# A gate's row loaded behind five adding loads, and new lists of attention pieces, in a two-block transformer kernel

## What is computed

```
log_f = log_sigmoid(f_logit + b_forget)
y_attn = forgetting_attention(q, k, v, log_f) * silu(z_attn)
merged = sigmoid(g_pool) * (y_pool @ w_up_pool) + sigmoid(g_attn) * (y_attn @ w_up_attn)
h = h + merged @ w_out
```

```
x = x + gt1 * (mixed @ w_o)
h = rmsnorm(x, g_norm2) * (1 + sc2) + sh2
x = x + gt2 * (square(relu(h @ w1)) @ w2)
```

## Time and profile before

| | us |
|---|---|
| median of three runs | 997.1 |
| the profiled execution | 995.43 |
| its span, first to last instruction | 993.6 |
| PE busy | 963.2 (97%) |
| weight loads of PE busy | 802.0 (81%) |
| DVE busy | 686.3 (69%) |
| ACT busy | 538.2 (54%) |
| POOL busy | 83.1 (8%) |

### The profile page before, as it was taken

The page is one execution under the profiler, slowest core; times in us unless marked ns, Lnnn a source line. Parts: engine busy times, 40 slices in busy tenths (PEclk is TensorE's granted clock), DMA queues, the critical chain, the costliest instruction groups (busy, mean ns, idle before and its releaser), DMA issues.

```text
span 993.6 us, 13125 instructions
## 1 busy us (share of the span) xinstructions
PE 963.2 (97%) x4712; PEld 802.0 (81%) x4712; DVE 686.3 (69%) x1269; ACT 538.2 (54%) x1053; POOL 83.1 (8%) x173
## 2 busy tenths in 40 slices
PE   8999999999999999999899999999599999999998
PEld 7878999888888888768788878788488888888886
DVE  6487888868788758767678886846244863674773
ACT  6458777753223445589786554356345634643520
POOL 4001001012112011100100000100100000000000
PEclk9999999999999999999999999999799999999999
DMA  8205231248779416452542234224968567583201
GB/s 296 80 23 183 65 106 55 86 188 326 281 287 335 165 71 246 160 158 83 139 142 70 66 98 177 85 85 98 230 208 205 134 208 191 122 237 127 84 32 53
DMA packets 36673, 148.69 MB, mean 150 GB/s; under 512 B 9193, under 2 KB 9193, under 8 KB 24706
## 3 DMA queue, kind: packets, MB, share of 16 engines
q1 hardware_dynamic: 23970, 101.41, 29.3%
q0 software_dynamic: 9568, 42.48, 16.3%
q10 hardware_dynamic: 3072, 3.98, 1.2%
HBM read 138.32 MB, written 5.27 MB: 145 GB/s over the span
## 4 chain that ended last, share of the span: by engine, by line
PE 81%; DVE 9%; ACT 4%; issue 3%; DMA 2%; POOL 0%; SPq 0%; ACTq 0%; DVEq 0%; POOLq 0%
PE psum L2091 24%; PE psum L2093 24%; PE psum L2092 24%; PE psum L2258 2%; PE psum L2237 2%; PE psum L2287 1%; PE psum L2290 1%; DVE wl L1237 1%; DVE two L1776 1%; DMA value_rows<-rows 1%; DVE hl L1277 1%; DVE two L1641 1%; DMA raw<-in_wall 1%; ACT wh L698 1%; DVE xt L1273 0%
## 5 line engine op out<-in xcount | busy, mean ns | idle before, releaser
L2091 PE MATMUL psum<-hh,wh 128*128 128x512 f32 (+1 forms) x720 | 274.0, 381 | 0.7 <-DVE hl L1277 0.6
L2093 PE MATMUL psum<-hh,wl 128*128 128x512 f32 (+1 forms) x720 | 267.3, 371 | 0.0
L2092 PE MATMUL psum<-hl,wh 128*128 128x512 f32 (+1 forms) x720 | 267.3, 371 | 0.0
L1237 DVE TENSOR_TENSOR wl<-raw,wh 128x512 fp32r<-128x512 f32 x328 | 213.9, 684 | 61.0 <-ACT wh L698 60.6
L698 ACT ACTIVATE wh<-raw 128x512 fp32r<-128x512 f32 x328 | 188.9, 620 | 103.9 <-PE psum L2093 68.2
L2091 PEld LDWEIGHTS psum<-hh,wh 128*128 128x128 f32 x720 | 135.3, 188 | 24.4 <-DVE hl L1277 1.4
L2093 PEld LDWEIGHTS psum<-hh,wl 128*128 128x128 f32 x720 | 135.2, 188 | 23.7
L2092 PEld LDWEIGHTS psum<-hl,wh 128*128 128x128 f32 x720 | 135.5, 188 | 21.2 <-issue 1.0
L2091 PE MATMUL psum<-wh,ah 128*128 128x512 f32 x224 | 89.8, 401 | 3.5 <-issue 3.5
L2092 PE MATMUL psum<-wl,ah 128*128 128x512 f32 x224 | 88.3, 394 | 0.0
L2093 PE MATMUL psum<-wh,al 128*128 128x512 f32 x224 | 88.3, 394 | 0.0
(11 more groups left out here) (335 smaller groups left out, 1633.9 us busy)
## 6 DMA issues: line engine op xcount, KB each, us to landing
raw<-in_wall SPq DMA_DIRECT2D x78, 1024.0 KB, 5.3
raw<-in_wall POOLq DMA_DIRECT2D x15, 1024.0 KB, 8.1
wa<-in_wada POOLq DMA_DIRECT2D x24, 512.0 KB, 5.9
gt<-in_wada POOLq DMA_DIRECT2D x20, 512.0 KB, 5.1
xt<-in_xcols SPq DMA_DIRECT2D x8, 264.0 KB, 8.2
cb<-c_rows SPq DMA_DIRECT2D x8, 264.0 KB, 3.6
x<-in_x SPq DMA_DIRECT2D x4, 512.0 KB, 10.2
x_kept<-x SPq DMA_DIRECT2D x4, 512.0 KB, 2.8
```

Of the source, the lines that this page charges most:

```text
L1237: e.tensor_tensor(home(w)[1][:, cs], raw_of(w, c), home(w)[0][:, cs].bitcast(F32), ALU.subtract).then_inc(v["wl"], 1)
L2091: e.matmul(out_, lh, rh, start=start, stop=False, skip_group_check=True)
L2092: e.matmul(out_, lh, rl, start=False, stop=False, skip_group_check=True)
L2093: return e.matmul(out_, ll, rh, start=False, stop=stop, skip_group_check=True)
```

## The change

`gate(1)` leaves its place before the loop over the quarters and goes behind the fifth adding load of the first quarter. The lists `PACE_F` and `PACE_S` are replaced; they hold as many pieces and as many empty beats as before (112 pieces in the first stage, 192 in the second), in the same order, begun in other steps. Of the returned blocks of values the first is subtracted one step later (88), the second nine steps later (97) and the fourth two steps earlier (120).

```diff
-PACE_F = [int(n) for n in ("00000000000000000011140110040102202010113010211101010115131000301121010101301202"
-                           "02000112030230300100300103023301100000110301311112112203021301123113200500330023")]
-PACE_S = [int(n) for n in ("11112111121111211112111121111211112002211200322014011101112010312102222120002304"
-                           "10211203011201010231200160011001211203331201110233120022213230100115031020203441"
-                           "3020305539041021021210001211")]
+PACE_F = [int(n) for n in ("00000000000000001004020200040012202010003300230102200014040001102022000210201301"
+                           "12000211030230300110200104012311000000202202411111110016002301040024300321022024")]
+PACE_S = [int(n) for n in ("11112111121111211112111121111211112013112210021031203200100012302201331210020202"
+                           "01202401003101221111102132111310211312310011034230102004204030201114130121213113"
+                           "1113216547312001203101101111")]
...
-        DV, DV_UPPER, DV_LOWER = (87, 88, 113, 122), (88, 89, 114, 123), (89, 90, 115, 124)
+        DV, DV_UPPER, DV_LOWER = (88, 97, 113, 120), (89, 98, 114, 121), (90, 99, 115, 122)
...
                 e.tensor_tensor(r, r, half[:, 0:1], ALU.pow).then_inc(g["rs3"], 1)
-            gate(1)
...
                 e.wait_ge(v["wl"], 4 * (o + 3) + 4)
                 add(q, 3, a1)
+                if q == 0:
+                    gate(1)
```

## The result

The changed kernel takes 985.75 us, the median of four runs (983.57 to 986.84), against 999.0 (996.34 to 1001.13, four runs) of the kernel before on the same chip: a ratio of 0.9866, 95% interval 0.983 to 0.9902. The forecast was 979.5, range 975 to 985. It is faster, as foreseen, by 13.3 us instead of 17.4, and lies 0.75 us above the range. The forecast started from the three runs named at the top, median 997.1; a fourth took 1001.13 and moved the median to 999.0, so part of the 13.3 us is that start. The profiled execution took 984.85 with a span of 983.1; before it was 995.43 and 993.6, so the span lost 10.5 us where the sum had 17.4.

What follows compares the result with a forecast made beforehand. PE was taken as the bound, so only its idle or slow stretches pay. Gate's row −15.4 and lists −2.0 us took the span from 993.6 to 976.2 and the median from 997.1 to 979.7, stated as 979.5, range 975 to 985.

Steps and rivals of the forecast that it cites:

- The gate's row: MLP's first quarter: with the row behind the adding loads, PE's gaps before P7 and P6 go; −15.4 us, at least 9.
- (c): First quarter: one gap stays because P6's weights are late again, with the slow clock behind; 988.4 us, chance 0.05.
- (d): First quarter: adding loads wait for their plain loads anyway, so nothing moves; 995 to 997 us, chance 0.02.
- (e): Second attention stage: new bursts delay VectorE's weight conversions and PE waits at units of weights; slower, 1001 us, chance 0.03.
- The lists: Attention stages: same work begun in other steps, so only waits differ; −2.0 us in sum, ends −5 and +3.
- The copy `low<-low` holds S8.3 of step 33, which stays where it was: 0: Second attention stage, step 33: the score's wait for its copy of keys stays unchanged; 0 us.
- The returned block comes at about 492 in either case: Second stage: steps 80 to 88 hold ten pieces in both lists, so VectorE is free before T13.3 is turned.
- T13.1: Turn in the second stage, begun in step 94 instead of 91: its 2.0 us of lateness goes; floor of gain 0.
- The wait of S10.3 for `al<-al`: Score of step 49, held 1.0 us by a copy of keys, now begun in step 50; −0.6 us.
- The last head's turns of the first stage: Steps 130 and 131: turns spread one to a step, passing ScalarE's table load; −0.4 us, between −1.3 and +0.7.
- The other waits for `ptl`: Attention stages: last head's turns −0.4 us against +1.0 us for new dense places in steps 40, 85, 169 and 170.
- Rival (a): Attention stages: the lists give nothing or cost up to 3 us; 981.7 to 984.7, say 983 us, chance 0.25.

Runs made afterwards that it cites:

- e1: Changed kernel with the old lists and DV steps, so only the gate's row is moved; 982.09 us, ratio 0.9849 to the kernel before.
- e6: Changed kernel with POOL's small stores of the first gate's row moved behind the last memset, to about 494 us; 982.17 us, ratio 0.9864 to the kernel before.
- e4: The changed kernel run again, unedited, beside the other runs; 985.44 us, ratio 0.9884 to the kernel before.
- e3: Changed kernel with T11.0 and S12.0 begun in step 76 as in the old list, not 75; 982.67 us, ratio 0.9856 to the kernel before.
- e2: Kernel before with the new lists and DV steps, the gate's row left where it was; 1001.3 us, ratio 1.0044 to the kernel before.
- e5: Changed kernel with the old lists and the first gate's small stores moved behind the memsets, some 500 us; 983.75 us, ratio 0.9874 to the kernel before.
- e9: Changed kernel with the old lists and the first gate's small stores moved behind V19.0, about 571 us; 979.54 us, ratio 0.9834 to the kernel before.
- e10: Changed kernel with its new lists and the first gate's small stores moved behind V19.0, about 571 us; 979.63 us, ratio 0.9836 to the kernel before.

## Why the prediction came out as it did

**The gate's row: right.** Forecast −15.4 us, by the distance of the plain loads 15.46, by e1 15.1 (997.19 to 982.09). The adding loads went out at 646, 661 and 669 us instead of 642, 655 and 664; the 4.9 us of the stages ahead are the difference, for in e1 they are at 642.40, 655.80 and 664.03. P7's and P6's weights were in time, the gate's row at 706 delayed nobody, the clock stayed up. Rivals (c), (d) and (e) did not occur.

At this place the Trainium skill's rule ("DMA: Bandwidth & Descriptors", "Issuing engines are not separate DMA queues") was kept out of the sum because the load it would stretch had time. It was not stretched: P1's plain load landed in 5.0 us after (issued at 667.68) and in 4.9 before. The adding load issued at 669.06 beside it took 9.2 us, against a median of 8.1 before, which agrees with the rule. The same rule bears on the place where I did not apply it: SP's copy of keys and POOL's small stores. The traces agree in that the copy took 4.7 us to landing beside the hole and 2.5 with the stores away (e6). But they show no packet of the stores in transfer during the hole, so what they show is more than interleaving, and what the rule does not say is that 2 KB can go with 2 to 3 us in which next to nothing moves.

**The lists: wrong.** Forecast −2.0, measured +4.9 in the profiled execution and +3.4 by e4 against e1. Two steps failed.

First, "The copy `low<-low` holds S8.3 of step 33, which stays where it was: 0". The score stayed, the copy's landing did not. I priced the wait by where its consumer stands in the list, and not by what else was in transfer when the copy was. The term was +3.85 us of waiting, with a stretch at clock 0.93 behind it. The old trace held the warning: the copy's last packets moved just ahead of a hole, as the row of transfers before shows.

Second, "The returned block comes at about 492 in either case". I compared the number of pieces in steps 80 to 88, and VectorE's steps, but the block's time is set ten steps earlier and on other engines: step 75's turn on ScalarE, the keys behind it, SP's queue behind their copies, the stores, the return load. It came at 497 in the change; beyond the stage's shift of 2.1 us that is 3 us late, and T13.1 waited 3.31 us instead of none. With the one step put back (e3) the block comes at 495, T13.1 waits 0.51, and 2.8 us return.

**The small terms.** The wait of S10.3 for `al<-al` went, as foreseen (no such line after). The last head's turns of the first stage gave −0.5 (foreseen −0.4). The other waits for `ptl` were foreseen as trading, +0.6 in all (−0.4 and +1.0): that holds, eight with 4.4 us after (7.7 − 3.3) against seven with 3.7. The four terms as measured, +3.9 for `low`, +1.4 for T13.1, −1.0 for `al` and +0.7 for the rest, are +5.0 where the sum had −2.0; the span lost 4.9. What the lower clock behind S8.3 cost is not priced apart.

**The rivals.** Rival (a), the lists give nothing or cost up to 3 us, was the nearest; its end of 984.7 is 1.05 us below the measured median, since both failures came together. My reason against it, that the largest wait had a cause that the new steps avoid, was wrong in its second half: they avoid it at its consumer and bring it back at its source.

**What stays open.** Why the copy finishes ahead of the hole with one list and behind it with the other, though both are the same up to there; what the small stores do that halts all transfers, and which of the two does it (in e3 the hole begins at about 425.5 us, ahead of the second store's issue at 427.31); and why the first quarter's gap was longer in e2.

## What to carry to other kernels

When an order of work is shifted, follow each awaited transfer back to the instruction that starts it, through every in-order queue between (here ScalarE, then SP), and compare both orders there; the consumer's step tells only who will feel it. Look at the windows of the DMA for holes, and ask which awaited transfer ends just ahead of one: such a copy cost four microseconds here when it came to lie behind the hole. A stall that is moved is not removed: move small stores to a stretch in which no transfer is awaited, and look there first.

## What was not expected of the hardware

Two stores of 2 KB each, in 4-byte elements, took 8.4 and 11.6 us from issue to landing after, and between them, from about 425 us on, the traffic of all 16 DMA engines was close to zero for 2 to 3 us. The eight weight packets of 8 KB that had begun just before took 2.8 to 3.0 us each (before 2.5 to 3.2), while the longest in the same place took 1.1 us in e5 and e6 with the stores elsewhere. The traffic stopped only with the stores there, in all eight profiles with them and in neither of these two. POOL's second such store was held 7.95 us at its issue after and 8.10 before. Moved to 570 us, the same two stores cost nothing that could be measured, in e9 or e10.
